# Two stacked transformer blocks on one core: row block by row block over the stage boundaries, and the order of the stages

## Chip, core and metric

One core of a Trainium2 chip runs the whole program. The metric is the device time of one execution in microseconds. Before the change it is 1826.72 us, the median of three runs (1819.81 to 1829.87).

## The reference, cut to what matters

All arithmetic is in float32. 256 rows of 1024 columns pass four layers of a first block and two of a second.

```python
for i in range(4):                                   # kinds A, B, C, A
    q, k, v, (qi, wi, ki), qm = split(x @ w_in)      # 12 heads of 64; indexer in kind A alone
    mix = own_attention(q, k, v)                     # A: 64 chosen keys, B: dilated, C: causal
    mo = memory_attention(qm, mem_n @ w_mem_kv[i])   # 4 heads over 256 memory rows
    x = layer_norm(ALPHA * x + concat(mix, mo) @ w_out[i], ln1)
    x = layer_norm(ALPHA * x + swiglu(x, w_gate_up[i], w_down[i]), ln2)   # 2816 hidden columns
for i in range(2):
    shift, scale, gate = split(silu(c) @ w_ada[i] + b_ada[i])
    h = rms_norm(x, norm_g[i]) * (1 + scale) + shift
    rq, rk, rv, rg, sq, sk, sv, sg = split(h @ w_in2[i])                  # 8 blocks of 512
    y = concat(retention(rq, rk, rv) * silu(rg), stick_breaking(sq, sk, sv) * silu(sg))
    x = x + gate * (y @ w_out2[i])
return rms_norm(x, final_g)
```

## The kernel before, in words

**Tiles.** The rows are two row blocks (rb 0 and 1) of 128. All weights come as 266 tiles of 128 partitions by 2048 columns (1 MB) from a packed array, in the order in which they are used; SyncE loads them into a ring of three (`RAW`, `sync_program`, L1614). A float32 product is made of three products of operands cut to a high and a low part (`products`, L604 to 607). So each weight tile is split once: ScalarE writes the high part (L898), VectorE the low part (L1077), into rings of `RING` = 3 split tiles. A slot comes free when row block 1 has been multiplied by its tile. Activations are treated alike: TensorE turns a row block in two halves of four 128-column chunks (`xt`, L640 to 667), ScalarE writes the high part (L908), VectorE the low one (L1104).

**Products.** A block of 512 output columns takes two tiles ("halves" of the 1024 inner rows). `block` (L197) multiplies tile 0 by row blocks 0 and 1, then tile 1 by 0 and 1; with `late`, row block 0 is first done with tile 0 and the late work (turning row block 1) stands after it. Each such product of a tile and a row block is 12 matrix instructions. Results go to two PSUM banks in turn (`gemms`), to two pairs of banks (`wide`), and turned rows to two more banks (`tr`).

**Order.** `Plan` writes one list of steps, and each engine runs its part of every step strictly in that order. A second stream, the background, is woven in by hand: `step_background` takes one step of it, at two places in each block, and `drain` takes all that is left. Units of attention are pipelined three deep (`pipelined`, L232). Nothing is placed by cost.

**A layer of the first block** (`first_layer`, L419): index columns and a narrow tile (kind A), projections 0 to 2, 4 and 3 of 512 columns; rotary and turned heads, the indexer and its eight rounds of top-8 are background. After projection 4 comes a drain, and the attention units (scores, softmax, turned probabilities, weighing) become background of projection 3. Then the units of row block 0 are finished, `xt` of the mixed rows, one product of `w_out`, the units of row block 1 are drained in `late` (L471), and the other seven products follow. `residual_norm` (L363) adds, normalises (stats L1150, gain L1188, power on POOL L1567, bias L1200) and turns both row blocks with no product between, except that the memory keys and values of the next layer (`memory_products`, L272) are made inside the second norm. `feed_forward` (L384) takes eleven steps of 256 hidden columns: an up block of two tiles, silu and product (`gate`, L994 and L1377), turned hidden rows (`turn_h`, L799, L1003, L1383) in one buffer, and one down tile. 24 further tiles of `w_ada_2` are only summed on VectorE (L1093).

**The second block** (`second_layer`, L526): root mean square (L1026, L1413), modulation by three rows (L815, L1018, L1403; L1422 and L1426), then projections 0, 1, 2 with rotary (a drain after each of the last two), then retention heads and after them stick-breaking pairs as background of projections 4, 5, 6, 3, 7. A pair is: scores (L848), abs, exp and log on ScalarE (L1040 to 1044), a sum over later keys (L1487, then L860), exp (L1052), weighing (L876). Then gates, turn and `w_out_2` in two blocks, and `add_gated` (L1504).

**Loads on POOL's queue** (`gpsimd_program`, L1535): norm gains and biases in two slots (L1553), constants, and POOL also computes the power for each norm.

Of the kernel before, what the change touches and what calls it, by code (L numbers as in the profile page):

```python
# [16 lines left out]
P = 128  # L17
# [33 lines left out]
RING = 3  # L51
# [83 lines left out]
Xt = namedtuple("Xt", "gen rb uses")  # L135
# [12 lines left out]
class Plan:  # L148
# [3 lines left out]
    def __init__(self, gemm, wide, tr):  # L152
        self.gemms, self.wide, self.tr = gemm, wide, tr
        self.steps, self.tiles, self.split = [], [], 0
        self.xt_uses, self.xt_last, self.before, self.gens = {}, {}, {}, []
        self.blocks, self.turns, self.last_unit, self.unit_of = {}, {}, {}, []
# [11 lines left out]
    def split_up_to(self, t):  # L168
        while self.split <= t:
            self.add("split", self.split)  # L170
            self.split += 1
# [5 lines left out]
    def xt(self, gen, rb):  # L177
        uses = (self.tr.take(), self.tr.take())
# [3 lines left out]
        self.xt_uses[gen, rb] = uses  # L182
        self.add("xt", Xt(gen, rb, uses))
# [8 lines left out]

    def drain(self):
# [3 lines left out]
    def block(self, name, layer, cols, gen, ring="gemm", late=None, then=None, what="half"):  # L197

        uses = [(self.gemms if ring == "gemm" else self.wide).take() for _ in range(RB)]
        t = [self.tile(name, layer, cols, what, 4 * half) for half in range(2)]  # L200
        self.split_up_to(t[0] + 2)
        self.gemm(t[0], 0, 0, gen, ring, uses[0])
        if late:
            late()
            self.gemm(t[1], 0, 1, gen, ring, uses[0])
            self.gemm(t[0], 1, 0, gen, ring, uses[1])
            self.split_up_to(t[1] + 2)
        else:
            self.gemm(t[0], 1, 0, gen, ring, uses[1])
            self.step_background()  # L210
            self.split_up_to(t[1] + 2)
            self.gemm(t[1], 0, 1, gen, ring, uses[0])
        self.gemm(t[1], 1, 1, gen, ring, uses[1])
        if then:
            then(uses, t[1])
        self.step_background()
        return uses, t[1]

    def evacuate(self, where, uses, tile, silu=False):
        for rb in range(RB):  # L220
            self.blocks[where, rb] = uses[rb]
            self.add("evac", Evac(where, rb, uses[rb], tile, silu, "act" if rb == 0 or silu else "dve"))
# [8 lines left out]
    @staticmethod  # L231
    def pipelined(units):  # L232
        waiting, middle, oldest = list(units), None, None
        while waiting or middle or oldest:
# [4 lines left out]
            oldest, middle = middle, new  # L239
            yield  # L240
# [13 lines left out]
    @staticmethod  # L254
    def followed(unit, act):
        yield from unit
        act()
# [5 lines left out]
    def memory_work(self):  # L263
        for rb in range(RB):
# [3 lines left out]
            self.add("bias", ("mem", rb))  # L268
            self.xt(("mem",), rb)
            yield  # L270

    def memory_products(self, layer):  # L272
        uses = [self.gemms.take() for _ in range(RB)]
        for half in range(2):
            t = self.tile("w_mem_kv", layer, 0, "half", 4 * half)
            self.split_up_to(t + 2)
            for rb in range(RB):
                self.gemm(t, rb, half, ("mem",), "gemm", uses[rb])
            self.step_background()
            yield  # L280
        self.evacuate(("mem", layer), uses, t)

    def turn_memory(self, layer):
        for rb in range(RB):
            self.turn("mk", layer, rb, range(2), "dve")

    def ada_tile(self):
# [3 lines left out]
        self.split_up_to(t + 2)  # L291
# [5 lines left out]
    def indexer_work(self, layer):  # L297
# [18 lines left out]
        for n in range(TOPK // 8):  # L316
            self.add("top8", (layer, n))
            if n % 3 == 2:
# [3 lines left out]
    def turn_heads(self, layer, what):  # L322
# [1595 lines left out]
```

## Time and profile before

| what | value |
| --- | --- |
| median of three runs | 1826.72 us |
| the profiled execution, its own time | 1820.88 us |
| its span, first to last instruction | 1819.0 us |
| TensorE busy | 1670.5 us (92%) |
| VectorE busy | 1090.0 us (60%) |
| ScalarE busy | 743.6 us (41%) |
| mean granted TensorE clock | 0.955 |
| mean DMA rate | 163 GB/s |

The span is that of one execution; 1.9 us of its time lie outside it. Busy times are sums over an engine's instructions. The granted clock is the mean over the span of TensorE's clock as a share of 2.4 GHz; it takes the values 1.0 and 0.5 alone here.

### The profile page before, as it was taken

Reading aid. Unit: us, or ns where it says so; the run is one execution under the profiler, and the core shown is the slowest. Engines: PE = TensorE matmul, PEld = TensorE weight load, DVE = VectorE, ACT = ScalarE, POOL = GpSimd, SP = SyncE. Lnnn points to the kernel's source line nnn. Section 1 sums busy time; section 2 is a strip of 40 time slices with the busy share of each in tenths; the row PEclk is TensorE's granted clock in tenths of the full one; section 3 lists DMA queues with packets and bytes.
Section 4 is the critical chain, followed back from the end, with each engine's and each line's share of the span. In section 5 each row is a group of like instructions: output and inputs, shape, how many; then the busy total and the mean of one; then the engine's idle time right before and its main releaser. Section 6 shows DMA issues by size and latency. Waiting matters only on the chain.

```text
span 1819.0 us, 19290 instructions
## 1 busy us (share of the span) xinstructions
PE 1670.5 (92%) x7900; PEld 1348.3 (74%) x7900; DVE 1090.0 (60%) x1470; ACT 743.6 (41%) x879; POOL 45.7 (3%) x74
## 2 busy tenths in 40 slices
PE   6888899999988999998899999888999979899987
PEld 5666778878767888786688878666788858776866
DVE  4854566557566566664666557836555667456634
ACT  4434344334433334344343333443343434654372
POOL 1000000000000000000000000000000000000000
PEclk8998899999999999999899999979999989998999
DMA  8341266655324565551266555313456535233421
GB/s 299 135 139 47 93 223 221 227 200 217 116 79 153 210 242 219 208 185 47 94 230 231 208 208 208 127 59 119 168 209 236 214 110 183 107 114 126 170 88 46
DMA packets 43111, 296.32 MB, mean 163 GB/s; under 512 B 4996, under 2 KB 5124, under 8 KB 8976
## 3 DMA queue, kind: packets, MB, share of 16 engines
q1 hardware_dynamic: 38592, 279.99, 42.1%
q0 software_dynamic: 4000, 14.00, 2.4%
q8 instruction: 62, 1.02, 0.2%
q10 hardware_dynamic: 432, 1.11, 0.2%
q14 instruction: 25, 0.20, 0.0%
HBM read 294.03 MB, written 1.05 MB: 162 GB/s over the span
## 4 chain that ended last, share of the span: by engine, by line
PE 79%; DVE 11%; ACT 6%; issue 2%; DMA 1%; POOLq 0%; SPq 0%; DVEq 0%; ACTq 0%; POOL 0%
PE psum L605 22%; PE psum L607 22%; PE psum L606 22%; DVE w_low L1077 3%; PE psum L628 2%; PE psum L787 2%; ACT w_high L898 2%; PE psum L665 2%; ACT work L971 1%; PE psum L799 1%; PE psum L769 1%; DVE neg_max L1333 1%; PE psum L718 1%; DMA w_raw<-in_weights 1%; PE psum L860 1%
## 5 line engine op out<-in xcount | busy, mean ns | idle before, releaser
L1077 DVE TENSOR_TENSOR w_low<-w_raw,w_high 128x2048 fp32r<-128x2048 f32 x242 | 552.1, 2290 | 378.8 <-ACT w_high L898 378.5
L605 PE MATMUL psum<-w_high,xt_high 128*128 128x512 f32 (+1 forms) x1536 | 618.5, 403 | 16.6 <-DVE w_low L1077 8.6
L607 PE MATMUL psum<-w_high,xt_low 128*128 128x512 f32 (+1 forms) x1536 | 606.1, 395 | 0.0
L606 PE MATMUL psum<-w_low,xt_high 128*128 128x512 f32 (+1 forms) x1536 | 605.3, 394 | 0.0
L898 ACT ACTIVATE w_high<-w_raw 128x2048 fp32r<-128x2048 f32 x242 | 459.9, 1911 | 254.6 <-PE psum L607 248.7
L605 PEld LDWEIGHTS psum<-w_high,xt_high 128*128 128x128 f32 x1536 | 296.4, 193 | 80.6 <-issue 13.6
L607 PEld LDWEIGHTS psum<-w_high,xt_low 128*128 128x128 f32 x1536 | 295.3, 192 | 62.7
L606 PEld LDWEIGHTS psum<-w_low,xt_high 128*128 128x128 f32 x1536 | 296.4, 193 | 57.1
L605 PE MATMUL psum<-w_high,ht_high 128*128 128x512 f32 x352 | 138.2, 393 | 6.3 <-DVE ht_low L1383 6.3
L607 PE MATMUL psum<-w_high,ht_low 128*128 128x512 f32 x352 | 137.8, 391 | 0.0
L606 PE MATMUL psum<-w_low,ht_high 128*128 128x512 f32 x352 | 137.7, 391 | 0.0
L994 ACT ACTIVATE arena<-psum 128x256 f32<-128x256 f32 x88 | 33.4, 384 | 243.4 <-PE psum L607 243.4
L1377 DVE TENSOR_TENSOR arena<-arena,psum 128x256 f32<-128x256 f32 x88 | 36.6, 420 | 97.6 <-ACT arena L994 97.6
L605 PEld LDWEIGHTS psum<-w_high,ht_high 128*128 128x128 f32 x352 | 66.4, 189 | 21.5 <-issue 7.9
L908 ACT ACTIVATE xt_high<-psum 128x512 fp32r<-128x512 f32 x64 | 36.1, 598 | 111.8 <-PE psum L665 111.8
L1003 ACT ACTIVATE ht_high<-psum 128x512 fp32r<-128x512 f32 x44 | 26.3, 598 | 131.1 <-PE psum L799 131.1
L971 ACT ACTIVATE work<-psum,neg_max 128x256 f32<-128x256 f32 (+3 forms) x112 | 49.9, 458 | 66.4 <-DVE neg_max L1333 66.4
L607 PEld LDWEIGHTS psum<-w_high,ht_low 128*128 128x128 f32 x352 | 66.5, 189 | 13.9
L606 PEld LDWEIGHTS psum<-w_low,ht_high 128*128 128x128 f32 x352 | 66.5, 189 | 13.7
L1567 POOL TENSOR_TENSOR norm_rstd<-norm_rstd,half_neg 128x1 f32<-128x1 f32 (+1 forms) x32 | 24.9, 781 | 1742.6 <-DVE norm_rstd L1152 1416.6
L1104 DVE TENSOR_TENSOR xt_low<-psum,xt_high 128x512 fp32r<-128x512 f32 x64 | 42.3, 688 | 37.7 <-ACT xt_high L908 37.2
L1093 DVE SCALAR_TENSOR_TENSOR arena<-w_raw,c_col,arena 128x512 f32<-128x512 f32 x84 | 63.1, 752 | 2.6
(201 smaller groups left out, 1382.0 us busy)
## 6 DMA issues: line engine op xcount, KB each, us to landing
w_raw<-in_weights SPq DMA_DIRECT2D x266, 1024.0 KB, 4.8
norm_params<-in_ln_g POOLq DMA_DIRECT2D x8, 512.0 KB, 4.0
norm_params<-in_ln_b POOLq DMA_DIRECT2D x8, 512.0 KB, 5.3
x_rows<-in_x SPq DMA_DIRECT2D x2, 512.0 KB, 4.6
arena<-in_mem POOLq DMA_DIRECT2D x2, 512.0 KB, 19.7
norm_params<-in_norm_g POOLq DMA_DIRECT2D x2, 512.0 KB, 3.8
out_rows<-x_rows ACTq DMA_DIRECT2D x2, 512.0 KB, 2.6
mem_kv<-in_decay POOLq DMA_DIRECT2D x1, 768.0 KB, 4.8
```

The lines of the kernel that those rows point to most:

```text
L605: e.matmul(dst, a_hi, b_hi, start=first, stop=False)
L606: e.matmul(dst, a_hi, b_lo, start=False, stop=False)
L607: return e.matmul(dst, a_lo, b_hi, start=False, stop=last)
L628: m = e.matmul(dst, left, right, start=banks[i] not in banks[:i], stop=banks[i] not in banks[i + 1:])
L665: m = e.transpose(psum[:, K.tr.place(n), c * P:c * P + P], src[:, (4 * g + c) * P:(4 * g + c + 1) * P], K.ident[:, :])
L787: m = e.matmul(psum[:, to, n * w:n * w + w], K.probt[slot][:, c * P:c * P + P], rows[:, kb, c0:c0 + w], start=kb == 0, stop=kb == nk // P - 1)
L898: e.activation(K.w_hi[:, g % RING, :], K.w_raw[:, r, :], ACT.Copy).then_inc(K.high.hit(t), 1)
L971: m = e.activation(dst, src, ACT.Exp, bias=K.negmax[:, slot, n:n + 1], accum_out=K.expsum[:, slot, n:n + 1])
L1077: e.tensor_tensor(K.w_lo[:, s, :], K.w_raw[:, r, :], K.w_hi[:, s, :].bitcast(F32), ALU.subtract).then_inc(K.taken.hit(t), 1)
L1093: m = e.scalar_tensor_tensor(out=acc, in0=w, scalar=c, in1=acc, op0=ALU.mult, op1=ALU.add)
L1104: e.tensor_tensor(lo[at], psum[:, K.tr.place(n), :].rearrange("p (c s) -> p c s", s=P), hi[at].bitcast(F32), ALU.subtract).then_inc(K.tr.s ...
L1377: e.tensor_tensor(K.ff_h[:, j.rb, :], K.ff_silu[:, j.rb, :], bank[:, FF_STEP:BLK], ALU.mult).then_inc(K.gemms.sem(j.use), 1)
```

## The change

What the diff does, part by part:

- `RING` goes from 3 to 5 split tiles; a split is no longer asked for before a tile is used, but one is owed for each product on row block 1, and `split()` places at most one of these at a time, after a product.
- `group` takes two blocks (four tiles) together: row block 0 through all columns of the first, then of the second, then row block 1 likewise. After each product a given action stands (a split, a background step, a turn, a drain). Groups are used for the first two projections of a layer (not in layer 0), projections 4 and 3, both halves of `w_out`, the first two steps of the feed-forward, and in the second block for projections 4 and 5, 7 and 3, and `w_out_2`.
- Each norm of a row block stands straight after that row block's last product, and its turn (`xt`) after the third product of the other row block or of the next group.
- The feed-forward turns its hidden rows one step later, into four buffers (`ht_hi`, `ht_lo`); down tiles come three steps later, and the last four are held together and taken row block by row block.
- All four layers' memory keys and values are made at the start, written to DRAM (`park`) and read back one layer at a time (`load_kv`). Norm parameters have one slot.
- Rotary and turned heads go by row block; the second block's order is projections 4, 5, 6, 0, 1, 2, then 7 and 3: stick-breaking runs one background step in two products beside 6, 0, 1 and then retention beside 7 and 3. `decay` is loaded once a layer.
- Buffers move in the arena; transposed heads, mask and rotary tables lie elsewhere.

The core of it:

```diff
-RING = 3
+RING = 5
...
+    def split(self, n=1):
+        for _ in range(min(n, self.owed)):
+            self.owed -= 1
+            self.add("split")
...
     def gemm(self, t, rb, half, gen, ring, use, kind="block"):
         self.add("gemm", Gemm(t, rb, half, gen, ring, use, kind))
+        self.owed += rb
...
+    def on(self):
+        self.split()
+        self.step_background()
+    def block(self, name, layer, cols, gen, then, what="half"):
+        uses = [self.gemms.take() for _ in range(RB)]
+        for half in range(2):
+            t = self.tile(name, layer, cols, what, 4 * half)
+            for rb in range(RB):
+                self.gemm(t, rb, half, gen, "gemm", uses[rb])
+                if half:
+                    then(rb, uses[rb], t)
+                self.on()
+    def group(self, blocks, gen, after):
+        t = [[self.tile(name, layer, cols, what, 4 * half) for half in range(2)] for name, layer, cols, what, _ in blocks]
+        for rb in range(RB):
+            for n, (*_, then) in enumerate(blocks):
+                use = self.gemms.take()
+                for half in range(2):
+                    self.gemm(t[n][half], rb, half, gen, "gemm", use)
+                    if half:
+                        then(rb, use, t[n][half])
+                    after[rb][2 * n + half]()
```

The memory at the start, and the order of layer 0:

```diff
+    def memory(self):
+        for rb in range(RB):
+            self.xt(("mem",), rb)
+        for layer in range(len(KINDS)):
+            self.block("w_mem_kv", layer, 0, ("mem",), self.evacuate(("mem", layer)))
+            for rb in range(RB):
+                self.turn("mk", layer, rb, range(2), "dve")
+            self.add("park", layer)
+        self.add("load_kv", 0)
...
+        if layer == 0:
+            self.beside(self.memory_norm())
+            self.block(w_in, at, 3 * MIX, gen, qi[-1])
+            narrow()
+            self.memory()
+            self.block(*proj(0)[:3], gen, proj(0)[-1])
```

The end of a layer's attention and the first norm (`sums` adds the residual and, after the second half, the norm of that row block):

```diff
+        self.group([proj(4), proj(3)], gen, [[self.on] * 3 + [attend], [self.on] * 4])
+        while (mix, 0, 1) not in self.xt_uses:
             self.step_background()
...
+        def rest():
+            self.split()
             self.drain()
+            if layer < LAST:
+                self.add("load_kv", layer + 1)
+            self.xt(mix, 1, (0,))
+        def end():
+            self.split()
+            self.xt(mix, 1, (1,))
+        def turned():
+            self.xt(("ff", layer), 0)
+            self.split()
+        self.group([("w_out", layer, h * BLK, "half", sums(h)) for h in range(2)], mix,
+                   [[self.on, self.on, rest, end], [self.split, lambda: None, turned, lambda: None]])
```

The end of the feed-forward (`steps` are the last four):

```diff
+        for rb in range(RB):
+            for step in steps:
+                down(step, t[step], rb)
+                if rb == 0:
+                    self.split()
+                    if step == FF_STEPS - 3:
+                        turn(FF_STEPS - 1)
+                elif step == FF_STEPS - 2:
+                    self.next_rows(layer, 0)
+                elif step != FF_STEPS - 1:
+                    self.split()
+            for h in range(2):
+                self.add("residual", Residual(out, rb, h, t[FF_STEPS - 1], "wide", acc[rb], h == 1))
+            self.norm(out, rb)
+            if layer == LAST:
+                self.add("rms", (0, rb))
+                self.add("modulate", (0, rb))
```

The second block:

```diff
+        self.group([proj(4), proj(5)], gen, [[self.split, self.split, late, self.split],
+                                             [self.split, turn("sq", 0, "act"), turn("sk", 0, "dve"), self.split]])
...
+        self.beside(stick_work())
+        project(6)
+        project(0)
...
+        project(1)
+        self.drain()
+        self.add("load_decay", layer)
...
+        project(2)
+        self.drain()
...
+        self.group([proj(7), proj(3)], gen, [[self.on] * 3 + [gate(0)], [self.on] * 3 + [gate(1)]])
+        self.xt(mix, 0)
...
+        self.group([("w_out_2", layer, h * BLK, "half", sums(h)) for h in range(2)], mix,
+                   [[self.split, self.split, lambda: self.xt(mix, 1), self.split],
+                    [self.split, lambda: None, turned, lambda: None]])
```

## Rows read from the trace of the kernel before

**Rows 1.** Busy times of the page, chain that ended last, and the core's span with its clock.

```profile
PE 1670.5 (92%) x7900; PEld 1348.3 (74%) x7900; DVE 1090.0 (60%) x1470; ACT 743.6 (41%) x879; POOL 45.7 (3%) x74
...
PE 79%; DVE 11%; ACT 6%; issue 2%; DMA 1%; POOLq 0%; SPq 0%; DVEq 0%; ACTq 0%; POOL 0%
...
core 0: 1819.0 us, clock 0.955
```

**Rows 2.** Waits of TensorE: instruction, what it waited for, us in total, times, longest us.

```profile
PE psum L665 <- DVE x_rows L1200: 18.8, 4, 4.7
...
PE psum L860 <- DVE arena L1487: 13.7, 4, 4.4
...
PE psum L787 <- ACT work L987: 13.1, 8, 4.0
...
PE psum L799 <- DVE arena L1377: 9.7, 4, 2.4
...
PE psum L605 <- DVE ht_low L1383: 6.3, 4, 1.6
...
PE psum L665 <- DVE arena L1200: 3.5, 2, 2.1
...
PE psum L718 <- DVE mem_kv L1214: 2.0, 1, 2.0
```

**Rows 3.** Windows: stretch, length, busy us of each engine, granted clock, DMA share, GB/s.

```profile
0.00:128.00 128.00, 102.15 (x466) 81.98 (x466) 87.19 (x201) 49.45 (x49) 12.21 (x26) 0.93 0.57 196
128.00:182.00 54.00, 44.69 (x290) 36.88 (x291) 23.06 (x33) 23.98 (x78) 0.00 (x0) 0.86 0.16 58
182.00:228.00 46.00, 39.36 (x156) 31.85 (x154) 26.24 (x31) 14.84 (x14) 1.59 (x2) 0.83 0.25 92
226.00:404.00 178.00, 174.01 (x779) 140.99 (x778) 105.53 (x92) 72.64 (x66) 0.00 (x0) 1.00 0.59 218
1081.00:1188.00 107.00, 96.95 (x472) 78.55 (x473) 82.03 (x184) 40.86 (x37) 4.83 (x8) 0.97 0.48 176
1564.00:1618.00 54.00, 47.03 (x246) 37.40 (x244) 23.61 (x38) 37.45 (x36) 2.54 (x3) 0.94 0.26 93
```

**Rows 4.** Timeline of TensorE, two stretches: start, us, instruction, tiles, shape.

```profile
40.12 0.63 PE L607 MATMUL psum<-w_high,xt_low 128*128 128x512 f32 x1
40.55 0.63 PE L605 MATMUL psum<-w_high,xt_high 128*128 128x512 f32 x1
...
47.17 0.39 PE L606 MATMUL psum<-w_low,xt_high 128*128 128x512 f32 x1
47.40 0.39 PE L607 MATMUL psum<-w_high,xt_low 128*128 128x512 f32 x1
```

**Rows 5.** Costliest groups of the page: splits of the weight tiles on VectorE and ScalarE.

```profile
L1077 DVE TENSOR_TENSOR w_low<-w_raw,w_high 128x2048 fp32r<-128x2048 f32 x242 | 552.1, 2290 | 378.8 <-ACT w_high L898 378.5
...
L898 ACT ACTIVATE w_high<-w_raw 128x2048 fp32r<-128x2048 f32 x242 | 459.9, 1911 | 254.6 <-PE psum L607 248.7
```

**Rows 6.** Timeline of VectorE at the first norm of layer 0, row block 0.

```profile
203.26 0.68 DVE L1167 SCALAR_TENSOR_TENSOR x_rows<-x_rows,psum 128x512 f32<-128x512 f32 x1
...
205.22 1.41 DVE L1188 SCALAR_TENSOR_TENSOR x_rows<-x_rows,norm_mean_var,norm_params 128x512 f32<-128x512 f32 x2
...
208.34 1.41 DVE L1200 SCALAR_TENSOR_TENSOR x_rows<-x_rows,norm_rstd,norm_params 128x512 f32<-128x512 f32 x2
```

**Rows 7.** Timeline between first and second block: ScalarE, VectorE, TensorE.

```profile
1479.00 1.06 ACT L1026 ACTIVATE work<-x_rows 128x1024 f32<-128x1024 f32 x1 [11.41 <-DVE x_rows L1200]
...
1483.68 0.69 DVE L1426 TENSOR_TENSOR work<-work,norm_params 128x512 f32<-128x512 f32 x1
...
1484.42 1.12 PE L665 MATMUL psum<-ident,work 128*128 128x128 f32 x4 [10.17 <-DVE work L1426]
```

**Rows 8.** Timeline of VectorE, the memory's norm of row block 0.

```profile
43.57 1.28 DVE L1158 BATCH_NORM_STATS2 norm_stats<-arena 128x6 f32<-128x512 f32 x2
...
45.39 1.43 DVE L1188 SCALAR_TENSOR_TENSOR arena<-arena,norm_mean_var,norm_params 128x512 f32<-128x512 f32 x2
```

More of the change, by code:

```diff
@@ L224, in turn, with evacuate, then @@
+    def evacuate(self, where, silu=False):
+        def then(rb, use, tile):
+            self.blocks[where, rb] = use
+            self.add("evac", Evac(where, rb, use, tile, silu, "act" if rb == 0 or silu else "dve"))
+        return then
     def turn(self, what, layer, rb, chunks, by):
@@ L405, in feed_forward, with late @@
+        def late():
+            self.xt(gen, 1)
+        self.group([("w_gate_up", layer, step, "up", gate(step)) for step in range(2)], gen,
+                   [[self.split, self.split, late, self.split], [self.split] * 4])
         turn(0)
-        for step in range(1, FF_STEPS):
-            up(step)
-            if step == 1 and layer == LAST:
+        for step in range(2, FF_STEPS):
+            self.block("w_gate_up", layer, step, gen, gate(step), "up")
+            if step == 2 and layer == LAST:
@@ L409, in feed_forward @@
                 self.add("load_gain", 0)
                 self.modulation(0, range(4))
[L411 to L422 removed]
+            turn(step - 1)
@@ L549, in second_layer, with proj, project, late @@
-        sticks[-2] = self.followed(sticks[-2], lambda: self.add("ret_gate", layer))
-        project(0, lambda: self.xt(gen, 1))
-        self.background.append(self.turn_retention(layer, 0))
+        gen, mix = ("sin", layer), ("sout", layer)
+        def proj(c):
+            return "w_in_2", layer, c * BLK, "half", self.evacuate(("proj2", layer, c), c % 4 == 3)
+        def project(c):
+            self.block(*proj(c)[:3], gen, proj(c)[-1])
+        def late():
+            self.xt(gen, 1)
+        def turn(what, rb, by):
+            def after():
+                self.split()
+                self.turn(what, layer, rb, range(4), by)
+            return after
@@ L571, in second_layer @@
-        self.block("w_out_2", layer, 0, mix, late=lambda: self.xt(mix, 1), then=first_sums)
-        uses, t = self.block("w_out_2", layer, BLK, mix, "wide")
-        for rb in range(RB):
-            self.add("add_gated", Gated(layer, rb, 1, t, "wide", uses[rb]))
+        rets = [self.retention(layer, h) for h in range(RET_H)]
+        self.beside(self.pipelined(rets))
+        if layer + 1 < DEPTH_2:
+            self.modulation(layer + 1, range(4))
+        else:
+            self.add("load_final")
@@ L669, in gemm @@
+        for c in range(4):
+            m = e.transpose(psum[:, K.tr.place(j.use), c * P:c * P + P], src[:, (4 * g + c) * P:(4 * g + c + 1) * P],
+                            K.ident[:, :])
+        m.then_inc(K.turned.hit(j.use), 1)
     def gemm(j):
```

674 lines of the change are left out of this document (323 added, 351 removed).

## The prediction, made before the change was run

> **What bounds the kernel now.** I read first the page's busy shares and the granted clock, then the table of waits, then a table of windows by stage, and last the timelines around three boundaries.
>
> TensorE is busy for 1670.5 of 1819.0 us, and its instructions fill 79% of the chain that ended last [rows 1]. So nothing but TensorE's own time counts: its work, its waits, and the time in which it runs at the lower of its two clocks. The waits and the tail together are 1819.0 - 1670.5 = 148.5 us. The mean granted clock is 0.955 [rows 1]. With levels of 1.2 and 2.4 GHz that is 2 x 0.045 x 1819 = 164 us at the lower one.
>
> What a clock level costs is seen in two pairs of neighbouring 512-column products: 0.23 us from start to start at 2.4 GHz (47.17 to 47.40), 0.43 us at 1.2 GHz (40.12 to 40.55) [rows 4]. One tile on one row block is twelve of these, 2.73 us at the full clock; four such products, the half of a group, are 10.9 us. If TensorE had work in all of the 164 us they would cost 82. In the two windows with the lowest clocks (0.86 and 0.83) it idles for 9.3 + 6.6 = 16 us of 100 [rows 3], so I take 84% of 82: 69 us.
>
> The waits are in few places [rows 2]. Four of 4.7 us stand at the first norm of each layer (behind the last addition of a bias, line 1200), four of 2.4 at the first turn of the hidden rows (L1377), four of 1.6 at the last (L1383). The stick-breaking drains give 13.7. The attention drains hold the 13.1 behind L987 and much beside: the first one has 54.0 - 44.7 = 9.3 us idle, the other three 6.8 to 9.1 alike. A feed-forward with both of its turns in it (226 to 404 us) idles 178.0 - 174.0 = 4.0 us, which are these 2.4 and 1.6, at clock 1.00 [rows 2, 3]; between them nothing is to be had, and most of the products lie there.
>
> **The change part by part.** The products stay the same in number, so their time at full clock stays. All sums are against the profiled execution, 1820.9 us, which is 5.8 below the median of the three runs.
>
> *First norm, four layers.* The norm of row block 0 moves beside four products of row block 1. Its chain on VectorE is 205.22 + 1.41 - 203.26 = 3.4 us up to the gains, plus 1.4 for the biases: 4.8 [rows 6]. That is under 10.9, so 4 x 4.7 = 18.8 go. But the second half of the attention rows of row block 1 is turned after that norm in VectorE's order. Its low part is ready 4.8 + 0.7 us after row block 0's last product; TensorE gets there after a turn of 0.6 and one product of 2.7, and waits 2.2. That is 4 x 2.2 = 9 back. In row block 1's norm, the next group's fourth tile is split behind the chain, at 4.8 + 2.3 = 7.1 us, and wanted at 8.2: nothing. Term: +10.
>
> *First turn of the hidden rows.* Two steps of columns are done before it, so the 9.7 us of L1377 go; with four buffers and the last four down tiles held, the 6.3 of L1383 go too. At the second norms, chains end about when they are wanted; I take 1 us each, 3 in all, back. Term: +13.
>
> *Attention.* The background of a layer takes 9 steps (12 in the dilated layer). Before, 7 (10) of them stand without a product between them; after, 3 (6), by my count of the calls. Idle time of 34 us (9.3 as in rows 3, and the others) halves: +17.
>
> *Fourth layer's indexer.* Its stretch idles 10 us [rows 3], behind VectorE. The change leaves it fewer products to hide in (14 in place of 18) but spreads the top-8 rounds: +2.
>
> *From the first block to the second.* Now 10.2 us of wait [rows 7]. After: row block 0's chain is 4.8 + 1.4 for a second sum, then square to first modulated half. That took 1484.4 - 1479.0 = 5.4 us with 1.5 of other work between [rows 7], so 3.9: ready at 10.1, the second half at 11.5. TensorE asks at 8.2 (three products in). Then the low parts queue behind two splits, 4.6 [rows 5]. Row block 1 repeats this with one split in the way. I add 1.9 + 0.8 + 2.0 for the first and 4.6 for the second: 9.3. Term: +1.
>
> *Second block.* The stick-breaking pairs step once in two products beside five blocks: the window from 1564 loses its 54.0 - 47.0 = 7 us [rows 3], twice, 14. Back come a drain of 1 us for them, one of 1.5 for retention, and 3 at the end: both gates of row block 1 (estimate 1.9) stand on VectorE before the low part of the turned rows that the next product needs. 11 for two layers. Term: +3. The last norm of row block 0 and the modulations placed earlier: +3.
>
> *Start.* The first 128 us idle for 128.0 - 102.2 = 26 us [rows 3]. The memory's norm moves beside the first block. In VectorE's order the evacuation of row block 1's index columns now stands behind two sets of stats and gains (1.6 + 1.4 each, [rows 8]), one bias and two splits: 6 + 1.4 + 4.6 = 12 us, while TensorE has 2.7 of narrow products on row block 0. I count 9.5 of wait, 2 more for the turned memory. Four memory blocks each end in a turn that waits for an evacuation, 2.0 as in [rows 2], three of them new: 6. Against that 3.5 (L1200, arena) and some 5 of the old drain go. Term: -9. At the three layer ends that these blocks used to fill, the products of row block 1 stand in for them, so nothing is gained or lost there.
>
> *Clock.* The lower level follows waits of some microseconds and the drains. I keep 7 us of cost at the start, 4 in each attention, 5 between the blocks, 6 elsewhere: 34 in place of 69. Term: +35. Bounds: 0 if every fall stays, 60 if all but the start's go.
>
> *Without cost.* Parking and reloading keys and values is 0.5 MB eight times, and decay 0.75 MB once more, on POOL's queue. The feed-forward moves 218 GB/s at a DMA share of 0.59 [rows 3], and the reloads have a whole layer; uncovered, each would cost some 4 us. POOL's powers stand behind these waits only where they have been met. Splits are as many. Five split tiles let two more tiles wait ready; a group holds four, so in it one is ahead.
>
> Sum: 10 + 13 + 17 + 2 + 1 + 3 + 3 - 9 + 35 = 75. 1820.9 - 75 = 1746, and 5.8 above that for the median: **1752 us**. Bounds of the parts: attention 5 to 28, start -20 to 0, clock 0 to 60, the new waits (9 + 3 + 9.3 + 11) from none to twice as much.
>
> **The rivals.** *The clock stays down as often.* The waits left are shorter but as many: attention steps between single products, a turn before each group. For it: at 1564 to 1618, 7 us idle went with a clock of 0.94 only, but 9.3 us idle in 54 went with 0.86 [rows 3], so small steps matter. Against: the feed-forward's waits of 2.4 and 1.6 us leave it at 1.00 [rows 3]. The sum without the clock term: 1752 + 35 = 1787. The Trainium skill ("TensorE: Matmul & The Clock Gate", section "A second HAM failure mode: psum-queue depth-cycling") tells of a kernel in which "the PE micro-idles between MM groups frequently enough that HAM oscillates"; by that rule this rival would hold, and the row at 1.00, with its two short waits, speaks against it here. Chance 0.15.
>
> *The waits I add do not appear.* If VectorE runs ahead everywhere, 9 + 3 + 9 + 11 and some 15 of the start and clock are saved: 1752 - 47 = 1705. For: VectorE is busy for 105.5 of 178 us in the feed-forward [rows 3], and for less in the attentions. Chance 0.15.
>
> *Slower: VectorE falls behind in every group.* In a row block 1 phase of 10.9 us it has up to four splits of 2.29 and a norm of 4.8, 14 us; a group holds four of five tiles, so a late split reaches TensorE at once. Price: one split chain, 1.91 + 2.29 = 4.2 us [rows 5], in each of some 25 groups (4 + 3 x 5 in the first block with the last downs, 6 in the second): 105, which gives 1857. It decides once a group loses 3.4 us, since (1836 - 1752) / 25 = 3.4. Against: two of the four splits stand after the norm, in the next phase. Chance 0.06.
>
> *The change only moves the waits.* The drains still wait for softmax and stick chains one after another, since each engine takes its steps in a fixed order; then term after term stays: about 1820. Chance 0.06.
>
> **How the numbers follow.** Forecast 0.58, with 1725 to 1780 as its own range. Range 1705 to 1795: it takes in the fast rival and the clock rival, and leaves out the last two and the far ends, some 0.2. A measurement of this kernel can tell about 0.5% from no change (1818 to 1836). Faster by more: 0.90; within: 0.04; slower: 0.06.
>
> **What would show it.** In the profile after, the waits for the second bias of the norms fall from four of 4.7 us to next to none; the wait on the first turn of the hidden rows is gone; short waits on the low part of turned rows appear at the output projections; a wait of about 10 us stands near 34 to 44 us from the start, released by the copy of index rows; a handful of waits, 9 us in all, stand between the two blocks. The mean clock is near 0.98. Products, splits and weight bytes are as before. I am wrong if TensorE's busy time does not fall by some 35 us, if the stick-breaking waits stay, or if waits for split tiles come up in every group.

## The result, and the profile after

| | before | after |
|---|---|---|
| median of the runs (4 and 4) | 1824.83 us | 1891.92 us |
| ratio, 95% interval | | 1.0367 [1.0329, 1.0404] |
| profiled execution, its span | 1820.9, 1819.0 us | 1888.0, 1886.2 us |

The change makes the kernel 3.7% slower; 1752 us, 4% faster, was forecast. The page of the changed kernel, its chain and its clock:

```profile
PE 1697.4 (90%) x7900; PEld 1358.3 (72%) x7900; DVE 1085.5 (58%) x1470; ACT 744.0 (39%) x875; POOL 46.6 (2%) x83
...
PE 67%; DVE 16%; ACT 9%; issue 6%; DMA 2%; POOL 0%; SPq 0%; ACTq 0%; DVEq 0%; POOLq 0%
...
core 0: 1886.2 us, clock 0.944
```

Against [rows 1] the instructions of TensorE are as many (7900), but they take 26.9 us more, at a lower clock, and the span holds 1886.2 - 1697.4 = 188.8 us without them, 40.3 more than the 148.5 of before. 26.9 + 40.3 = 67.2 is the whole difference of the spans. VectorE has no more to do than before (1085.5 for 1090.0 us), yet its share of the chain rises from 11% to 16%, ScalarE's from 6% to 9%. Their load did not grow, so their order is the first suspect.

The largest waits of TensorE in the changed kernel (instruction, what it waited for, us in total, times, longest):

```profile
PE psum L682 <- DVE xt_low L1176: 25.2, 15, 7.7
PE psum L793 <- DVE arena L1299: 19.1, 12, 4.8
PE psum L705 <- ACT arena L1013: 17.3, 10, 3.7
PE psum L844 <- DVE work L1418: 13.9, 4, 6.5
PE psum L682 <- DVE ada_rows L1466: 13.5, 12, 1.1
PE psum L682 <- DVE w_low L1150: 11.4, 4, 6.5
PE psum L934 <- DVE arena L1559: 10.8, 6, 4.2
PE psum L682 <- DVE work L1286: 7.8, 1, 7.8
```

The 18.8 us behind a norm's second bias and the 9.7 + 6.3 of the hidden rows [rows 2] are gone, as forecast. In their place stand waits for turned rows (L1176), rope (L1299), ScalarE's copies of turned heads (L1013) and normalised weights of the softmax (L1418). The waits of stick-breaking (L1559), which were to go, stay at 10.8 us, for 13.7 before. Waits for a split tile (L1150) are only four.

Where it happens is told by windows that begin and end at the same events in both kernels, each time TensorE turns the first rows for a new stage: start; layer 0's feed-forward; layer 1's attention; the fourth layer's indexer and attention; its feed-forward; the second block's first layer. Columns as in [rows 3]. The kernel before:

```profile
0.00:209.10 209.10, 169.28 (x846) 137.15 (x846) 126.42 (x255) 80.37 (x131) 13.41 (x28) 0.91 0.43 150
209.10:419.20 210.10, 205.35 (x906) 166.78 (x907) 128.51 (x120) 82.40 (x73) 3.04 (x5) 0.98 0.55 202
419.20:548.90 129.70, 116.50 (x574) 92.85 (x572) 79.80 (x135) 49.81 (x69) 2.29 (x4) 0.96 0.38 136
1099.00:1267.40 168.40, 146.15 (x784) 118.31 (x782) 105.39 (x219) 65.95 (x117) 3.43 (x6) 0.92 0.34 124
1267.40:1484.40 217.00, 202.16 (x870) 160.39 (x870) 130.15 (x130) 83.01 (x79) 6.92 (x11) 0.96 0.54 197
1484.40:1652.90 168.50, 157.81 (x741) 124.55 (x741) 97.32 (x140) 83.30 (x81) 3.67 (x5) 0.94 0.35 128
```

The changed kernel:

```profile
0.00:258.20 258.20, 207.81 (x990) 168.01 (x991) 142.87 (x266) 94.19 (x140) 15.01 (x31) 0.89 0.44 154
258.20:453.30 195.10, 191.57 (x859) 154.44 (x858) 121.20 (x115) 81.06 (x72) 2.21 (x4) 1.00 0.57 210
453.30:598.50 145.20, 120.15 (x570) 93.50 (x569) 79.86 (x134) 47.94 (x67) 2.74 (x5) 0.92 0.32 118
1128.70:1313.10 184.40, 155.56 (x780) 125.86 (x779) 106.67 (x218) 64.28 (x115) 3.33 (x6) 0.86 0.29 107
1313.10:1517.10 204.00, 197.65 (x868) 156.68 (x866) 122.04 (x120) 81.86 (x76) 5.64 (x10) 0.99 0.57 207
1517.10:1694.50 177.40, 152.06 (x684) 117.54 (x685) 94.85 (x138) 76.81 (x75) 4.68 (x6) 0.90 0.34 126
```

The start holds 144 more instructions (x990 for x846), three memory blocks of 10.9 us that left layers' ends; the feed-forward holds 47 fewer. So layer 0's feed-forward went from 210.1 - 10.9 = 199.2 to 195.1, 4 us better and at clock 1.00. The attention of layer 1, with as many instructions, went from 129.7 to 145.2: 11.9 us more idle (length less busy time: 13.2, then 25.1) and the rest, 3.6 us, TensorE's own time at a lower clock. The fourth layer's lost 16, the second block's 8.9 although it holds 57 instructions fewer. The loss sits where background steps stand beside products.

One attention step, in the changed kernel's timeline (start, us, engine, instruction, idle before it), ScalarE, VectorE, TensorE:

```profile
523.63 0.58 ACT L1045 ACTIVATE work<-psum,neg_max 128x384 f32<-128x384 f32 x1 [3.47 <-DVE neg_max L1405]
...
528.29 1.91 ACT L972 ACTIVATE w_high<-w_raw 128x2048 fp32r<-128x2048 f32 x1 [3.98 <-PE psum L684]
...
530.23 2.29 DVE L1150 TENSOR_TENSOR w_low<-w_raw,w_high 128x2048 fp32r<-128x2048 f32 x1 [6.30 <-ACT w_high L972]
...
532.82 0.29 DVE L1418 TENSOR_TENSOR work<-work 128x128 f32<-128x128 f32 x1
533.03 0.55 DVE L1405 TENSOR_REDUCE neg_max<-psum 128x1 f32<-128x384 f32 x1
...
523.13 0.47 PE L844 MATMUL psum<-ident,work 128*128 128x128 f32 x1 [6.52 <-DVE work L1418]
...
533.16 0.33 PE L844 MATMUL psum<-ident,work 128*128 128x128 f32 x1 [3.46 <-DVE work L1418]
...
542.81 0.47 PE L844 MATMUL psum<-ident,work 128*128 128x128 f32 x1 [3.46 <-DVE work L1418]
```

The exponential and its sum are done at 524.3. The normalisation needs only that, 0.7 us of VectorE. But both engines have a split next in their queues. The buffer of that tile is freed by the product that TensorE is running, so the high part starts at its end, 528.29, the low part at 530.23, and the normalisation comes after it, at 532.4. TensorE, which issued the scores of the next unit right behind the product, stands still for 3.46 us. Then it turns the weights and runs the next product, and the same begins again: one step in (542.81 - 523.13) / 2 = 9.8 us, where a product takes 2.7 at the full clock and TensorE's own work for the step under 2. Some 2 of the 9.8 are clock: after the waits these two products ran partly at the lower level and took 4.9 and 4.5 us. In the kernel before, a block has its background step first and its split behind it; the helper `on()` of the change has the split first.

### The profile page after: what moved, and what is told of

It reads as the page before. It is cut to its first block, busy times and chain, and to the rows that moved or that the text cites. A ratio compares the mean times of both kernels' runs of the same rounds, so it can differ in the third digit from the quotient of the medians.

```text
span 1886.2 us, 19314 instructions
## 1 busy us (share of the span) xinstructions
PE 1697.4 (90%) x7900; PEld 1358.3 (72%) x7900; DVE 1085.5 (58%) x1470; ACT 744.0 (39%) x875; POOL 46.6 (2%) x83
## 3 DMA queue, kind: packets, MB, share of 16 engines
q1 hardware_dynamic: 38592, 279.99, 40.3%
## 4 chain that ended last, share of the span: by engine, by line
PE 67%; DVE 16%; ACT 9%; issue 6%; DMA 2%; POOL 0%; SPq 0%; ACTq 0%; DVEq 0%; POOLq 0%
PE psum L682 19%; PE psum L684 19%; PE psum L683 19%; ACT w_high L972 6%; DVE w_low L1150 5%; PE psum L705 2%; PE psum L861 2%; DMA w_raw<-in_weights 2%; PE psum L873 1%; ACT work L1045 1%; PE psum L793 1%; PE psum L934 1%; PE psum L844 1%; PE psum L740 1%; DVE neg_max L1405 1%
## 5 line engine op out<-in xcount | busy, mean ns | idle before, releaser
L1150 DVE TENSOR_TENSOR w_low<-w_raw,w_high 128x2048 fp32r<-128x2048 f32 x242 | 553.2, 2290 | 432.3 <-ACT w_high L972 431.5
L682 PE MATMUL psum<-w_high,xt_high 128*128 128x512 f32 (+1 forms) x1536 | 628.4, 409 | 59.9 <-DVE xt_low L1176 25.2
L683 PE MATMUL psum<-w_low,xt_high 128*128 128x512 f32 (+1 forms) x1536 | 611.7, 398 | 0.0
L682 PEld LDWEIGHTS psum<-w_high,xt_high 128*128 128x128 f32 x1536 | 302.0, 197 | 145.3 <-issue 27.7
L684 PEld LDWEIGHTS psum<-w_high,xt_low 128*128 128x128 f32 x1536 | 299.8, 195 | 64.3
L683 PEld LDWEIGHTS psum<-w_low,xt_high 128*128 128x128 f32 x1536 | 301.5, 196 | 57.6
L682 PEld LDWEIGHTS psum<-w_high,ht_high 128*128 128x128 f32 x352 | 66.2, 188 | 12.5
L1001 ACT ACTIVATE arena<-psum 128x512 f32<-128x512 f32 x44 | 26.3, 597 | 117.9 <-PE psum L684 115.8
L1286 DVE COPY arena<-psum 128x512 f32<-128x512 f32 x36 | 24.8, 688 | 79.5 <-PE psum L684 79.5
L793 PE MATMUL psum<-ident,arena 128*128 128x128 f32 x192 | 33.1, 303 | 36.4 <-DVE arena L1299 19.1
## 6 DMA issues: line engine op xcount, KB each, us to landing
arena<-in_mem POOLq DMA_DIRECT2D x2, 512.0 KB, 19.1
```

Source lines behind the costliest of these rows:

```text
L682: e.matmul(dst, a_hi, b_hi, start=first, stop=False)
L683: e.matmul(dst, a_hi, b_lo, start=False, stop=False)
L684: return e.matmul(dst, a_lo, b_hi, start=False, stop=last)
L793: m = e.transpose(psum[:, K.tr.place(j.use), n * P:n * P + P], src[:, c * P:c * P + P], K.ident[:, :])
L1150: e.tensor_tensor(K.w_lo[:, s, :], K.w_raw[:, r, :], K.w_hi[:, s, :].bitcast(F32), ALU.subtract).then_inc(K.taken.hit(t), 1)
```

## The experiments

Theory A: the order in `on()`, split ahead of the background step, makes the loss. Rivals: B, the chains of attention (score, maximum, exponential, weight) are long in any order; C, VectorE is full and TensorE starves for tiles (the slower rival of the prediction); besides, smaller causes: the modulation rows' bank (A2), a copy at the start (A3), the gates. Ratios are to the kernel before, run on the same chip.

**1. The background step first.**

```
-        self.split()
         self.step_background()
+        self.split()
```

> Edit: at every step between two products the background step (softmax, rope, stick, memory work) stands ahead of the split of the next tile; nothing else moves. Theory A (a split is queued ahead of the background step and has to wait for the product just issued, so the ScalarE and VectorE parts of that background step, which wait for nothing, start some 4 us late and TensorE then waits for them): most of the waits of 3 to 7 us on scores, rope and stick copies go, 40 to 60 us of idle time and 10 to 20 us of slow clock with it; about 1835 us. Rival B (the drains are long because the chain from score to weight is long whatever the order of the queues): the waits stay, 1892 us within 8. Rival C (VectorE is simply too full and a late split now starves TensorE of tiles): the waits turn up at the products as waits for the low part of a split tile, 1890 us or above.

Measured: 1843.01 us, ratio 1.0133 [1.0088, 1.0179]. 2.3% of the 3.7 go: about 43 us. B as the whole cause falls, and so does C: waits for a split tile are still four, 15.5 us. But 1.3% of loss stays although the background step now stands first, as in the kernel before. Layer 1's attention idles 134.7 - 117.8 = 16.9 us here, for 25.1 in the changed kernel and 13.2 before:

```profile
PE 1673.1 (91%) x7900; PEld 1341.0 (73%) x7900; DVE 1085.6 (59%) x1470; ACT 742.2 (40%) x875; POOL 46.6 (3%) x83
...
443.90:578.60 134.70, 117.84 (x570) 92.12 (x569) 80.09 (x134) 47.40 (x67) 2.74 (x5) 0.94 0.35 127
```

Runs 5 and 10 look for the rest.

**2. One split fewer owed** (`self.owed = RING - 1`): each split's buffer was freed one product earlier.

> Edit: one split fewer is owed at the start, so that each split stands one pair of products later and its buffer was freed by an earlier product instead of the one just issued; its place ahead of the background step is kept. Theory A in its exact form (it is the wait for the product just issued that holds up the queue, not the split's own 1.9 and 2.3 us): nearly all of what the swap of the two brings is had here too, 1830 to 1850 us. If only the split's own length counts, the queue is as long as before: 1880 us or above.

Measured: 1862.40 us, 1.0232 [1.0187, 1.0278]. That is between the two cases and above the 1850 of theory A. The waits in the attentions fell (L1418 from 13.9 to 6.8 us, L1299 from 19.1 to 9.4), but another kind came up and takes back part of the gain:

```profile
PE psum L682 <- DVE w_low L1150: 44.3, 11, 7.9
```

Eleven waits for split tiles in place of four. The plan gives the likely reason: a group holds four of the five tiles, so little is ready ahead of it.

**3. and 4. Two small causes.** The modulation tile ahead of the down products; and the start's index columns of row block 1 copied by ScalarE.

```
             if step < FF_STEPS - 1:
+                if 2 < step < 9:
+                    self.ada_tile()
                 if step > 2:
...
-                if 2 < step < 9:
-                    self.ada_tile()
```

> Edit: in the feed-forward the modulation tile stands ahead of the two down products instead of behind them. Theory A2 (the modulation rows' evacuation is queued behind other work and holds the accumulator bank that the next up product wants, 12 times 1.1 us): the two products between cover it, so 13 us go, 1878 us. Rival: the bank is only freed when ScalarE or VectorE gets to it, and that comes later in any order: no change, 1892.

> Edit: row block 1 of the first block of columns for the indexer is evacuated by ScalarE instead of VectorE, at the start of the kernel. Theory A3 (the evacuation stands behind the memory's norm on VectorE and the narrow product waits for its buffer, 7.8 us): the wait goes, with part of the 24 us of slow clock that follows it: 8 to 15 us, 1880 us. Rival: the clock is low at the start for another reason, the wait alone goes or moves behind the memory's norm: 0 to 5 us, 1888.

Measured: 1875.25 us, 1.0314 [1.0262, 1.0366], and 1885.07 us, 1.0371 [1.0320, 1.0421]. The twelve waits for the modulation rows are gone, 13.5 us in the profile; the time is lower by 0.5%, which the intervals don't separate from the changed kernel. A3 is a miss: the ratio is that of the changed kernel (1.0367), and the wait moved behind the memory's norm, where there had been 1.4 us:

```profile
PE psum L740 <- DVE memt_low L1176: 10.7, 1, 10.7
```

**5. The first, the third, and the gates' splits behind the turn of row block 0.**

```
             def then():
-                self.on()
+                self.step_background()
...
                 self.add("ret_gate", (layer, rb))
+                if rb:
+                    self.xt(mix, 0)
+                self.split(2)
...
-        self.xt(mix, 0)
```

> Edits: the background step ahead of the split (first run), the modulation tile ahead of the down products (third run), and in the gated group of the second block the two gates and the turn of row block 0 ahead of the last two splits. If the three causes are separate costs they add: the first gives 43 to 49 us, the second 12 to 15, the third 6 of the 10.9 us of wait that stand at the second block's output projections: 1892 - 43 - 13 - 6 = 1830 us, still no gain on the kernel before. Rival: the waits removed are taken up by others behind them, 1840 or above.

Measured: 1816.41 us, 0.9984 [0.9967, 1.0001]. Better than the sum, but no gain on the kernel before. Its VectorE shows why. The maxima of three steps, and the split between two of them:

```profile
502.92 0.55 DVE L1407 TENSOR_REDUCE neg_max<-psum 128x1 f32<-128x384 f32 x1
...
506.06 2.29 DVE L1152 TENSOR_TENSOR w_low<-w_raw,w_high 128x2048 fp32r<-128x2048 f32 x1 [2.35 <-ACT w_high L974]
...
508.90 0.56 DVE L1407 TENSOR_REDUCE neg_max<-psum 128x1 f32<-128x384 f32 x1
...
515.48 0.55 DVE L1407 TENSOR_REDUCE neg_max<-psum 128x1 f32<-128x384 f32 x1
```

A step takes 6.0 and 6.6 us. Maximum (VectorE), exponential and high part (ScalarE), low part and normalisation (VectorE) go one after another: VectorE waits 2.35 us for the high part with the normalisation, which could go, queued behind it. TensorE waits 1.99 us for that in the second step; in the first it doesn't wait, since its product, partly at the lower clock, took 4.5 us.

**6. and 7. The lag again**, on top of run 5: everywhere, and only around the attentions and sticks.

> Edits of the run before with one split fewer owed at the start, in the whole kernel. Theory A: with the background step already ahead, the lag still spares the step that follows the split its wait for the product just issued; the drains' idle falls by 2 to 5 us in each of six, but in the groups, which hold four tiles, the waits of 3.5 and 2.8 us for a split tile come up that the second run had (about 35 us in all). About 1840 us; 1815 if the groups' waits had another cause.

> The three edits, and one split fewer owed only from the blocks before each attention (and the sticks) to the group after it, where it is caught up. Theory A: the gain of the lag in the drains without the waits in the groups: 10 to 20 us below the run with the three edits, 1812 to 1822 us. Rival: the drains wait for their own chain (score, maximum, exponential, turn, weigh) and not for a queue: same as the run with the three edits.

Measured: 1854.45 us, 1.0176 [1.0140, 1.0213], and 1817.00 us, 0.9978 [0.9959, 0.9998]. Everywhere it costs 1.9%, more than was expected (w_low waits again, 11 of them, 48.4 us). Only around the drains it gives nothing: the time lies in the range expected by theory A, but the gain of 10 to 20 us against run 5 is not there, so the rival holds. Once the background step is first, the product just issued is no longer what it waits for.

**8. The order of the change put into the kernel before.** First at every block's middle and end; then (9) only where a background step waits:

```
             self.gemm(t[0], 1, 0, gen, ring, uses[1])
+            if self.background:
+                self.split_up_to(t[1] + 2)
             self.step_background()
...
+        if self.background:
+            self.split_up_to(min(t[1] + 3, N_TILES - 1))
         self.step_background()
```

> The kernel before, with the split put ahead of the background step in each block (in the middle and at its end), as the change has it; nothing of the row block order changes. Theory A: the same waits come up here, at two places in a block instead of four and so about half as many as in the changed kernel: 15 to 35 us slower than the kernel before, 1835 to 1855 us by its median of 1820. Rival (the waits come from the new order of products and not from the queue): within 5 us of the kernel before.

> As the run before on the kernel before (split ahead of the background step), but only where a background step is waiting, so that no split comes ahead of a norm or a turn of rows at the end of a block, which that run did as well. Theory A: background steps beside products alone pay now; two in a block, some 4 us each where a wait shows: 15 to 60 us slower than the kernel before, 1835 to 1880. Rival: all of the 174 us that the run before lost came from the norms and nothing from the background steps: within 5 us of the kernel before.

Measured: 1994.59 us, 1.0978 [1.0928, 1.1028], and 1951.43 us, 1.0698 [1.0652, 1.0743]. The first also put splits ahead of norms, and was no clean test. The second is: with the products in their old order, the queue order alone costs 7%. The direction is theory A's, the size is over twice its upper end. The clock and the first wait of this kernel (13.7 us in [rows 2]):

```profile
core 0: 1960.1 us, clock 0.916
...
PE psum L864 <- DVE arena L1491: 33.7, 8, 4.9
```

TensorE's busy time rose by 60.9 us at that clock (1731.4 for 1670.5), the rest is idle time. Of the 141 us between the spans 78 lie in the two layers of the second block (168.5 and 166.1 us before, 205.7 and 206.6 here), and layer 0's feed-forward, which has next to no background steps, takes 210 us as before. Why it is 7% here where run 1 gave back 2.3% stays open.

**10. The low part one step later.** On top of run 5; a "low" in the list of steps is where VectorE does its part of the last tile:

```
         self.step_background()
-        self.split()
+        self.add("low")
+        if self.owed > 0:
+            self.owed -= 1
+            self.add("split")
```

> The three edits, and VectorE's part of a split (the low part) is issued one step later than ScalarE's: behind the next background step's normalisation and maximum instead of ahead of them. Seen in the run with the three edits: a background step beside a product comes every 6.0 to 6.6 us where the product and the step's own TensorE work take 4, because maximum (VectorE), exponential (ScalarE), high part (ScalarE), low part (VectorE), normalisation (VectorE) go one after another. Theory D (this round through both engines bounds the drains now): some 25 interleaved steps lose 1 to 2 us each with part of their slow clock: 1775 to 1800 us. Rival: the drains are held by the bare steps and other engines' chains: 1816 within 6.

Measured: **1748.86 us, 0.9589 [0.9555, 0.9623]**, the fastest of all, 4.1% below the kernel before. The direction is theory D's; the gain against run 5, 4.0% or some 70 us, is well over the 16 to 41 us expected. So the round through both engines cost more than the steps counted for it, or more steps than were counted.

**11. and 12. Which engine's place pays, and whether the kernel before gains too.** The high part ahead of the background step in kernel 10; the late low part in the kernel before.

> The run with the late low part, but with ScalarE's high part put ahead of the background step again, as the change has it. What pays then is ScalarE's wait for the product just issued and its 1.9 us ahead of exponentials and copies, VectorE is free of it. If ScalarE's place makes most of the loss of the change: 1790 to 1830 us. If VectorE's low part makes most of it: 1750 to 1770 us.

> The kernel before with one edit: where a background step is waiting, VectorE's part of a split comes behind it instead of ahead of it; order of the products and three split tiles as before. If the late low part alone makes the gain of the run with it (4% against the same order without it), this kernel too comes to 1760 to 1785 us and the row block order is worth little. Theory: it needs steps that stand beside products; before, 7 of a layer's 9 stand bare, so little changes: 1805 to 1825 us.

Measured: 1800.32 us, 0.9913 [0.9881, 0.9946], and 1810.52 us, 0.9946 [0.9921, 0.9971]. From 0.9589, ScalarE's place costs 3.2% of the kernel before and VectorE's (run 5) 4.0%: either half of a split in the way is enough. (In run 11 the low part of the tile before stands ahead of the step too, but its high part was done long ago, so ScalarE's place is nearly all that it tests.) The kernel before gains 0.5% by the late low part, the changed one 4.0% (run 5 to run 10). In these runs the row block order and the queue order pay only together. The five split tiles came with the row block order, and no run parts the two.

**13. Nothing but the split's place**, in the changed kernel.

> The changed kernel with one thing altered: each split's high part is issued behind the background step, its low part behind the next one. The modulation tile and the gates stay where the change has them. If the costs add (those two gave 26 us between the first run and the run with the three edits): 1749 + 26 = 1775 us, within 10, so 45 below the kernel before. Rival: the two other edits were needed for the gain: 1800 or above.

Measured: 1754.78 us, 0.9636 [0.9585, 0.9686]. This misses its range (1765 to 1785) on the fast side. The costs don't add: the modulation tile and the gates gave 1.5% on run 1, and here at most 0.5%, which the intervals of runs 10 and 13 don't separate from nothing. The trace shows part of the reason: the twelve waits for the modulation rows, which run 1 still has (13.5 us), are gone without that tile having moved. Its page, clock, and windows as above:

```profile
PE 1649.9 (94%) x7900; PEld 1330.3 (76%) x7900; DVE 1085.8 (62%) x1470; ACT 740.5 (42%) x875; POOL 46.5 (3%) x83
...
core 0: 1755.1 us, clock 0.971
```

```profile
0.00:232.40 232.40, 195.51 (x990) 159.84 (x991) 142.70 (x266) 93.56 (x140) 14.99 (x31) 0.94 0.48 170
232.40:423.30 190.90, 190.69 (x860) 154.67 (x859) 121.44 (x115) 81.08 (x72) 2.21 (x4) 1.00 0.61 216
423.30:550.20 126.90, 116.18 (x569) 92.12 (x568) 79.72 (x134) 47.31 (x67) 2.73 (x5) 0.96 0.38 137
1058.30:1221.80 163.50, 144.62 (x780) 116.90 (x779) 105.95 (x218) 63.60 (x115) 3.33 (x6) 0.93 0.33 123
1221.80:1424.70 202.90, 199.97 (x868) 158.24 (x866) 122.41 (x120) 81.75 (x76) 5.63 (x10) 0.97 0.56 207
1424.70:1580.70 156.00, 143.53 (x685) 112.67 (x686) 94.86 (x138) 76.38 (x75) 4.67 (x6) 0.96 0.40 143
```

And its step, on ScalarE and VectorE:

```profile
488.54 1.91 ACT L982 ACTIVATE w_high<-w_raw 128x2048 fp32r<-128x2048 f32 x1
...
487.29 0.56 DVE L1415 TENSOR_REDUCE neg_max<-psum 128x1 f32<-128x384 f32 x1 [0.83 <-PE psum L715]
...
488.23 2.28 DVE L1160 TENSOR_TENSOR w_low<-w_raw,w_high 128x2048 fp32r<-128x2048 f32 x1
...
491.71 0.55 DVE L1415 TENSOR_REDUCE neg_max<-psum 128x1 f32<-128x384 f32 x1
```

The low part of one tile (488.23) runs beside the high part of the next (488.54), and a step takes 491.71 - 487.29 = 4.4 us, at the full clock and with no wait of TensorE: 9.8, 6.3, 4.4 for the three orders of the same work, part of the first two being the lower clock.

## Why the prediction was wrong, step by step

**The step that failed** is in "Without cost": "Splits are as many." Their number was right (242 of 2.29 us, before and after); their place was not looked at. I had counted for the norms and the gates which splits stand ahead of them, and for the background steps, which are far more, I had not. It went wrong in two ways.

First, `on()` issues the split ahead of the background step, where it waits for the product just issued. Run 1 puts the step first, as in the kernel before: about 43 us come back, and 1843.01 are left, still 91 above the forecast.

Second, the term "Attention, +17" halves the idle time because more steps stand beside a product, and so takes such a step as free. But a split stands between two of them, and its handoff from ScalarE to VectorE lay in their chain: 6.0 to 6.6 us for a step in run 5. Only with the low part one step later (run 13) does the changed kernel come to 1754.78 us.

**That this is near the forecast of 1752 is luck.** The kernel before doesn't place the low part so, the change doesn't, and the forecast didn't assume it. Nor do all the parts fit. Of 1819.0 - 1755.1 = 63.9 us between the spans, 43.3 are idle time (148.5, then 1755.1 - 1649.9 = 105.2) and 20.6 TensorE's clock. Forecast were 40 and 35.

*First norm, +10, and hidden rows, +13.* Right. The waits on L1200 and L1377 are gone, and layer 0's feed-forward has 0.2 us idle in run 13, against 4.7. The waits of 2.2 on the low part at the four output projections came too; in run 13's timeline all four are 2.20, the first of them:

```profile
226.86 0.50 PE L692 MATMUL psum<-w_high,xt_high 128*128 128x512 f32 x1 [2.20 <-DVE xt_low L1186]
```
In the changed kernel itself part of this gain was lost again: the modulation rows, which I had not seen would hold a product's bank, gave 13.5 us of wait.

*Attention, +17, and the indexer, +2.* Wrong in the changed kernel, where layer 1 lost 11.9 us of idle time instead of gaining 4; in run 13 mostly absent. Layer 1's window idles 10.7 us for 13.2, and the 2.5 between them are the norm's 4.7 less the 2.2. So halving the steps that stand without a product gave nothing there, even where a step beside a product had become free. In layer 2 (15.2 us idle before, 9.0 in run 13) it gave 3.7, in the fourth layer, with the indexer, 0.9.

*First to second block, +1.* Before there were 10.2 us; in run 13 that turn of the rows waits 1.5, and the feed-forward of the fourth layer idles 6.4 us instead of 14.8, with three waits of 1.5 to 1.7 us following in the second block. Better than forecast.

*Second block, +3 and +3.* Wrong in the changed kernel (idle 10.7 us, then 25.3, in its first layer). There the gates stand behind three splits and one more, and the wait at the output projections is 7.7 us in the first layer (the longest of the waits on L1176 above) and 3.1 in the second, where 3 was said. The stick-breaking waits, whose staying I had named as a sign of being wrong, stayed. In run 13 they are next to nothing (0.7 us), and the whole second block idles 12.5 + 13.7 = 26.2 us for 29.0 before, 2.8 less where 6 less was said.

*Start, -9.* The wait on the narrow product came in the changed kernel, 7.8 us for 9.5, behind L1286. The turns behind the memory's blocks, forecast at 8 us in all, wait 6.6 us there for such a copy and 6.7 in run 13: about right. The start as a whole idles 50.4 us (39.8 before) and in run 13 36.9. Of the 13.5 us between the two, 8.2 lie behind the memory's blocks, in layer 0's attention, so most of what the order of the splits cost here lies there too.

*Clock, +35.* The changed kernel lost 26.9 us. The clock fell where the waits grew: 0.92 for 0.96 in layer 1's attention, 0.90 for 0.94 in the second block's first layer. The rival "the clock stays down" had the mechanism, as a consequence of waits that I had not forecast. With the waits gone the term is 20.6, inside its bounds of 0 to 60. The Trainium skill ("TensorE: Matmul & The Clock Gate", section "A second HAM failure mode: psum-queue depth-cycling") tells of a kernel in which frequent small idle times of TensorE between groups of products make the clock go up and down. Both sides are in these traces: a feed-forward with three waits of 1.1 us keeps 1.00, and layer 1's attention, with one wait of 6.5 us and two of 3.5 around single products, has 0.92.

*The slower rival.* It had the right sign and 0.06. Its mechanism, late splits that starve TensorE in each group, is not what happened: w_low waits are four before the lag of run 2 is put in. The splits were not late for TensorE; they made the softmax late. Eleven such waits in run 2 show that the rival's condition is near, though. The other slow rival, that the change only moves the waits (0.06), is nearer in mechanism: it names the fixed order in which each engine takes its steps. But it put that at no gain, about 1820, and priced no loss.

*The range*, 1705 to 1795, left out the right case, because no case in it put a price on the splits that stand between background steps. The place of the kernel before would not have saved it: run 1, at 1843, is outside too.

## What to carry to other kernels

Where two engines each take their steps in a written order, cost a step by what stands ahead of it in each queue and by what that is waiting for. Work that waits for the product just issued comes last, behind all that could already run (2.3% here). A preparation of two halves on two engines (high, then low part) has its second half one step later where a chain crosses the same engines (4.0% here, but 0.5% in the kernel before, where few such steps stand beside products). And test a reordering with its parts apart: here the new order of products gave +3.7% or -3.6%, by the place of the same splits.

## What the runs showed that was not expected

The same 242 splits and the same 7900 instructions of TensorE take 1755 or 1892 us, by the splits' place in the queues alone. The step beside a product took 9.8, 6.3 and 4.4 us. And idle time and clock went together over the whole change: 40.3 us of one and 26.9 of the other lost, 43.3 and 20.6 gained by run 13 against the kernel before. It is not a fixed price, though: from run 1 to run 5 the idle time fell from 164.2 to 142.6 us, 13.5 of it the short waits for the modulation rows in feed-forwards at a clock of 1.00, and TensorE's busy time only from 1673.1 to 1671.7. A wait must be priced with the clock that it takes where it stands.
